# Two hybrid transformer blocks on one core: memory attention that reads its four score banks directly, and an earlier first bias in the differential attention

## The chip, the cores and the metric
One core of a Trainium2 chip runs the whole program in one launch. The metric is the time of one execution on the device in microseconds (us), as the median of several runs. Engines are named as in the profile: PE (matrix products; PEld is its loading of weights), DVE (vector), ACT (scalar functions), POOL and SP (which issues the DMAs of the weights). PE's granted clock is given as a share of 2.4 GHz.

## What is computed
A sequence of 256 tokens with 1024 features goes through two blocks of two layers each, all in float32. The first block ("A") has differential attention, stick-breaking attention and a mixture of product-key experts; the second ("B") has a hybrid attention mixer, cross attention to a memory of 256 tokens, and an MLP. The change touches the softmax of two of these:

```python
# differential attention, per head and block of 128 queries
sc = einsum('bhmqd,bhmkd->bhmqk', dq, dk) * scale
sc = where(dist >= 0, sc - slopes * dist, -inf)
p = softmax(sc, axis=-1)
attn = p[:, :, 0] - lam * p[:, :, 1]
# memory cross attention: 4 heads of 64, no mask and no bias
s = einsum('bqhd,bmhd->bhqm', q, k) * DH ** -0.5
p = softmax(s, axis=-1)
o = einsum('bhqm,bmhd->bqhd', p, v)
```

## The kernel before
All weights come as a stream of tiles of 128 x 2048 values through a ring of four slots. SP loads a slot again when the semaphore `tile_done` says that PE has finished the tile that was in it. Most large products are made of a rounded high part and a low part of each weight: ACT copies a half tile of 1024 columns to `tile_h` (`act_high`), DVE subtracts it and writes the rest over the ring (`dve_low`, one call for the two halves of a tile), and PE adds three products (`pe_project`, `pe_up`, `proj_run`). PE works through its list in a fixed order written by hand; so do ACT and DVE. Semaphores are the only link between them.

Attention is cut into **units**: two heads (or the two maps of one differential head) and 128 queries. Three functions write the three engines' lists for a sequence of units:

- `pe_units` (line 404): the scores of units 0 and 1, then an optional `lead` of other work, then for each unit u: the **turn** (transposes of the probabilities into bank `ps[6]`, L423; it waits for DVE's `sm_p`), the scores of unit u + 2, a piece of **fill** (other products, if there are any), the **values** (probabilities times values; they wait for ACT's copy `pt_ev` of the turned bank), and a second piece of fill. The scores of a unit go to bank 4 or 5 in turn, so those of unit u + 2 wait until the maximum of unit u is there. Between the two halves of a unit's scores PE waits for its own first half (`sc_first`).
- `act_units` (line 444): the exponentials of unit u + 1 (L451: two activations that read S and add up their rows), then the copy of the turned bank of unit u (L465).
- `dve_units` (line 471): for each unit the **bias** (from the bank to the buffer S in SBUF; for a memory unit, which has none, a plain copy, L481) and the maximum over S (L491), then the reciprocal of the sum (L498) and the scaling of the exponentials (`plain_scale`, L509; `diff_scale`, L596 to L598), and an optional `after(u)`. The bias of unit u + 1 is ahead of the scaling of unit u. `step.after` makes DVE wait for its own last result.

There are eight differential units a layer in block A and four memory units a layer in block B. The memory units have no fill: their queries are ready when ACT has copied `ps[4]` to `xq` (L1785), and after the last of them PE goes on with the down product of the memory branch (`down_by_tokens`, L269), once ACT has copied the values' banks 0 and 1 (L1790). That product adds up in banks 0 to 3. Bank 6 holds the turned probabilities, banks 0 and 1 the values.

The differential units have fill: the projections 6 to 9 of the layer's input (`proj_run`, L854), of which six pieces are the `lead`. ACT rounds the tiles 1 to 7 and DVE makes their low parts before the first unit. In `dve_block1` (its loop `for j in range(1, 8)` is ahead of the units) low part 7 and the two small operations for lambda (L1188, L1189) come ahead of the first bias; low parts 8 and 9 come in `after(3)` and `after(5)`. Low part j has to wait for ACT's high part j, and ACT makes high part 7 after it has copied out projection 5.

DVE_A and DVE_B count DVE's own waits in a layer of each block.

Of the kernel before, what the change touches and what calls it, by code (L numbers as in the profile page):

```python
# [125 lines left out]

DVE_A, DVE_B = 128, 121


def program(nc, stream, x_in, consts, table, scratch, out):
    ctx = ExitStack()
    with ctx:
# [266 lines left out]
        sc_mm, sm_max, sm_exp, sm_p = sem("sc_mm"), sem("sm_max"), sem("sm_exp"), sem("sm_p")  # L401
        pt_mm, pt_ev, pv_mm = sem("pt_mm"), sem("pt_ev"), sem("pv_mm")

        def pe_units(pe, base, units, scores, values, fill=None, lead=None):

            def score(u):
                if u >= 2:
                    pe.wait_ge(sm_max, base + (u - 1))
                for m in range(2):
                    klen = units[u]["keys"]  # L410
                    last = scores(units[u], m, ps[4 + u % 2][:, m * 256:m * 256 + klen])
                    if m == 0:
                        last.then_inc(sc_first, 1)
                        pe.wait_ge(sc_first, base + (u + 1))
                last.then_inc(sc_mm, 1)

            def turn(u):
                pe.wait_ge(sm_p, base + (u + 1))
                if u >= 1:
                    pe.wait_ge(pt_ev, base + u)  # L420
                for m in range(units[u]["turned"]):
                    for kt in range(units[u]["keys"] // P):
                        last = nc.tensor.transpose(ps[6][:, (2 * m + kt) * P:(2 * m + kt + 1) * P],  # L423
                                                   E[:, u % 2, m, kt * P:(kt + 1) * P], ident)
                last.then_inc(pt_mm, 1)

            score(0)
            score(1)
            if lead is not None:
                lead()  # L430
            for u in range(len(units)):
                turn(u)
                if u + 2 < len(units):
                    score(u + 2)
                if fill is not None:
                    fill(u, 0)
                pe.wait_ge(pt_ev, base + (u + 1))
                for m in range(2):
                    last = values(units[u], m, PT[:, u % 2, m, :, :])
                last.then_inc(pv_mm, 1)  # L440
                if fill is not None:
                    fill(u, 1)

        def act_units(act, base, units, fill_out=None, after=None):
            def exps(u):
                act.wait_ge(sm_max, base + (u + 1))
                if u >= 2:
                    act.wait_ge(pt_mm, base + (u - 1))
                klen = units[u]["keys"]
                for m in range(2):  # L450
                    last = nc.scalar.activation(E[:, u % 2, m, 0:klen], S[:, u % 2, m, 0:klen], ACT.Exp,  # L451
                                                bias=negmax[:, u % 2, m:m + 1], accum_out=total[:, u % 2, m:m + 1])
                last.then_inc(sm_exp, 1)

            exps(0)
            for u in range(len(units)):
                if u + 1 < len(units):
                    exps(u + 1)
                if fill_out is not None:
                    fill_out(u)  # L460
                act.wait_ge(pt_mm, base + (u + 1))
                if u >= 2:
                    act.wait_ge(pv_mm, base + (u - 1))
                n, maps = units[u]["keys"] // P, units[u]["turned"]
                nc.scalar.activation(PT[:, u % 2, 0:maps, 0:n, :],  # L465
                                     ps[6][:, :].rearrange("p (m k q) -> p m k q", m=2, k=2)[:, 0:maps, 0:n, :],
                                     ACT.Copy).then_inc(pt_ev, 1)
                if after is not None:
                    after(u)

        def dve_units(dve, step, base, units, scale_probs, after=None):
            def bias(u):
                w = units[u]
                klen = w["keys"]
                dve.wait_ge(sc_mm, base + (u + 1))
                if u >= 2:
                    dve.wait_ge(sm_exp, base + (u - 1))
                raw = ps[4 + u % 2][:, :].rearrange("p (m k) -> p m k", m=2)[:, :, 0:klen]
                s = S[:, u % 2, :, 0:klen]
                if w["table"] is None:  # L480
                    last = nc.vector.tensor_copy(s, raw)  # L481
                elif w["minus"] is None:
                    for m in range(2):
                        last = nc.vector.scalar_tensor_tensor(s[:, m, :], raw[:, m, :], w["scale"], w["table"][m],
                                                              ALU.mult, ALU.add)
                else:
                    for m in range(2):
                        last = nc.vector.scalar_tensor_tensor(s[:, m, :], raw[:, m, :], w["minus"][m], w["table"][m],
                                                              ALU.subtract, ALU.add)
                step.after(last)  # L490
                nc.vector.tensor_reduce(negmax[:, u % 2, :], s, AX.X, ALU.max, negate=True).then_inc(sm_max, 1)  # L491
# [678 lines left out]
        def dve_block1(dve, l):  # L1170
# [10 lines left out]
            nc.vector.tensor_reduce(lamp, lam2.rearrange("p (a n) -> p a n", a=2), AX.X, ALU.add).then_inc(lam_sum, 1)  # L1181
            step.after(nc.vector.tensor_scalar(smA[:, 0:1], smA[:, 0:1], smA[:, 2:3], None, ALU.mult))
            dve_split_x(dve, 2 * l)
            for j in range(1, 8):
                dve_low(dve, A_PROJ, l * SPLIT_A - 1, 0, j)
            dve.wait_ge(lam_exp, l + 1)

            step.after(nc.vector.tensor_tensor(neglam, elam[:, 1:2], elam[:, 0:1], ALU.subtract))  # L1188
            step.after(nc.vector.tensor_tensor(neglam, neglam, smA[:, 1:2], ALU.subtract))  # L1189
            def low_after(u):  # L1190
                if u == 3:
                    dve_low(dve, A_PROJ, l * SPLIT_A - 1, 0, 8)
                if u == 5:
# [262 lines left out]
        for pair in range(2):  # L1456
            for qt in range(TT):
                mix_units.append(unit("fox", pair, qt, minus=[negcum[:, qt, 2 * pair + m:2 * pair + m + 1]
                                                              for m in range(2)]))
        mem_units = [unit("mem", pair, qt, keys=SEQ, table=None) for pair in range(2) for qt in range(TT)]  # L1460

        def b_scores(w, m, out):
# [43 lines left out]
        def pe_block2(pe, l):  # L1506
# [150 lines left out]
            arrived(pe, 2, l, B_XQ)  # L1657
            up_as_turned(pe, norm + 1, chunks(B_XQ), 4, lambda: norm_read(pe, norm + 1)).then_inc(tile_done, 1)
            pe.wait_ge(x_ev, l * 3 + 3)
            pe_units(pe, done_b + l * UNITS_B + len(mix_units), mem_units, b_scores, b_values)  # L1660
            pe.wait_ge(xo_ev, l * 2 + 2)
            arrived(pe, 2, l, B_XO)
            down_by_tokens([(slot(B_XO), lambda i, tt: xo[:, i, tt * P:(tt + 1) * P])], True)
# [16 lines left out]
        def act_block2(act, l):  # L1680
# [97 lines left out]
            def memory_out(i):  # L1778
# [5 lines left out]
            finished(act, 2, l, B_XQ)  # L1784
            nc.scalar.activation(xq, ps[4][:, :].rearrange("p (a n) -> p a n", a=2), ACT.Copy,  # L1785
                                 scale=HD ** -0.5).then_inc(x_ev, 1)
            act_units(act, done_b + l * UNITS_B + len(mix_units), mem_units)
            act.wait_ge(pv_mm, done_b + (l + 1) * UNITS_B)
            for b in range(2):
                nc.scalar.activation(xo[:, b, :], ps[b][:, 0:SEQ], ACT.Copy).then_inc(xo_ev, 1)  # L1790
# [7 lines left out]
        def dve_block2(dve, l):  # L1798
# [125 lines left out]
                                        sig[:, i, 2, :], ALU.add).then_inc(br_used, 1)  # L1924
            norm = 2 * LAYERS + 3 * l
            dve_norm(dve, step, norm, 2, l, B_LN1, B_MIX + 3)
            dve_units(dve, step, done_b + l * UNITS_B + len(mix_units), mem_units, plain_scale)
            dve_norm(dve, step, norm + 1, 2, l, B_LN2, B_XO)

            dve_split_x(dve, 2 * LAYERS + 2 * l + 1)  # L1930
# [241 lines left out]
```

## Time and profile before

| | |
|---|---|
| median of 3 runs | 3148.97 us (3147.49 to 3149.35) |
| the profiled execution's own time | 3148.95 us |
| its span, from first to last instruction | 3147.1 us |
| mean granted clock of PE | 0.978 |
| busy: PE, PEld | 3051.5 us (97%), 2638.1 us (84%) |
| busy: DVE, ACT, POOL | 1930.9 us (61%), 1301.5 us (41%), 8.2 us |
| read from HBM | 490 MB, 156 GB/s over the span |

The span is what the timeline covers; the 1.85 us between span and time lie around it. Times in rows are counted from the span's start. A busy PE can still run at half clock, which the busy share doesn't show.

### The profile page before, as it was taken

How to read it: one execution, taken by the hardware profiler on the slowest of the kernel's cores; microseconds unless marked ns; L12 is line 12 of the kernel's file. 1: busy time of each engine (PE TensorE's matmuls, PEld its weight loads, DVE VectorE, ACT ScalarE, POOL GpSimd, SP SyncE). 2: the span in 40 equal slices, each digit the busy share in tenths (PEclk: the TensorE clock that was granted, in tenths of full speed). 3: DMA queues.
4: the chain of work that ended last, by engine and by line, in shares of the span. 5: the costliest groups of instructions: out<-in, count | busy, mean ns of one | idle time of the engine just before them, and what ended most of it. 6: DMA issues, size and time to landing. Idle time of an engine off the chain costs nothing.

```text
span 3147.1 us, 52803 instructions
## 1 busy us (share of the span) xinstructions
PE 3051.5 (97%) x20490; PEld 2638.1 (84%) x20490; DVE 1930.9 (61%) x3611; ACT 1301.5 (41%) x2001; POOL 8.2 (0%) x10
## 2 busy tenths in 40 slices
PE   7999999999999999999999999999998999999898
PEld 7688889898897868888989899797776979777697
DVE  3489864787547548985578755745434564543456
ACT  4422444444444441244444444444424444442444
POOL 0000000000000000000000000000000000000000
PEclk9999999999999999999999999999998999999899
DMA  5244355544545334335553455452243545224354
GB/s 197 94 161 142 127 187 187 188 147 161 194 180 189 146 107 159 133 136 188 186 187 147 170 189 196 175 205 80 81 160 122 187 179 210 81 81 162 119 187 147
DMA packets 68018, 493.53 MB, mean 157 GB/s; under 512 B 7576, under 2 KB 7584, under 8 KB 8352
## 3 DMA queue, kind: packets, MB, share of 16 engines
q1 hardware_dynamic: 67568, 490.42, 43.0%
q8 instruction: 104, 1.70, 0.2%
q0 software_dynamic: 304, 1.06, 0.1%
q14 instruction: 42, 0.34, 0.0%
HBM read 490.39 MB, written 1.06 MB: 156 GB/s over the span
## 4 chain that ended last, share of the span: by engine, by line
PE 93%; DVE 3%; ACT 2%; issue 1%; DMA 0%; DVEq 0%; SPq 0%
PE ps L647 9%; PE ps L649 9%; PE ps L648 9%; PE ps L233 8%; PE ps L617 8%; PE ps L618 8%; PE ps L619 8%; PE ps L699 6%; PE ps L994 3%; PE ps L1008 2%; PE ps L269 2%; PE ps L1607 2%; PE ps L1634 2%; PE ps L250 2%; PE ps L854 1%; PE ps L295 1%
## 5 line engine op out<-in xcount | busy, mean ns | idle before, releaser
L763 DVE TENSOR_TENSOR ring_l<-ring,tile_h 128x1024 fp32r<-128x1024 f32 x648 | 764.8, 1222 | 675.2 <-ACT tile_h L718 671.2
L718 ACT ACTIVATE tile_h<-ring 128x1024 fp32r<-128x1024 f32 x644 | 645.6, 1051 | 533.4 <-PE ps L649 445.3
L617 PE MATMUL ps<-x_h,tile_h 128*128 128x256 f32 x2016 | 575.5, 285 | 0.6 <-issue 0.6
L618 PE MATMUL ps<-x_l,tile_h 128*128 128x256 f32 x2016 | 570.0, 283 | 0.0
L619 PE MATMUL ps<-x_h,ring_l 128*128 128x256 f32 x2016 | 569.9, 283 | 0.0
L617 PEld LDWEIGHTS ps<-x_h,tile_h 128*128 128x128 f32 x2016 | 386.4, 192 | 1.6 <-issue 1.4
L618 PEld LDWEIGHTS ps<-x_l,tile_h 128*128 128x128 f32 x2016 | 386.5, 192 | 0.2
L619 PEld LDWEIGHTS ps<-x_h,ring_l 128*128 128x128 f32 x2016 | 386.3, 192 | 0.0
L722 ACT ACTIVATE arena<-ps 128x512 f32 (+1 forms) x160 | 95.6, 597 | 466.1 <-PE ps L619 345.0
L647 PE MATMUL ps<-tile_h,w_even 128*128 128x512 f32 x640 | 249.5, 390 | 3.6 <-DVE w_even L788 3.6
L647 PE MATMUL ps<-tile_h,w_odd 128*128 128x512 f32 x640 | 249.4, 390 | 0.6 <-DVE w_odd L788 0.6
L648 PE MATMUL ps<-ring_l,w_even 128*128 128x512 f32 x640 | 249.1, 389 | 0.0
L649 PE MATMUL ps<-tile_h,w_odd 128*128 128x512 f32 x640 | 249.0, 389 | 0.0
L649 PE MATMUL ps<-tile_h,w_even 128*128 128x512 f32 x640 | 249.0, 389 | 0.0
L648 PE MATMUL ps<-ring_l,w_odd 128*128 128x512 f32 x640 | 249.0, 389 | 0.0
L233 PE MATMUL ps<-xT,ring 128*128 128x256 f32 x1088 | 237.5, 379 | 0.0
L233 PEld LDWEIGHTS ps<-xT,ring 128*128 128x128 f32 x1088 | 205.5, 190 | 27.3
L784 DVE TENSOR_TENSOR arena<-arena (+1 forms) x160 | 159.9, 1000 | 4.1 <-ACT arena L1142 4.1
L647 PEld LDWEIGHTS ps<-tile_h,w_even 128*128 128x128 f32 x640 | 120.1, 188 | 29.3 <-DVE w_even L788 3.0
L647 PEld LDWEIGHTS ps<-tile_h,w_odd 128*128 128x128 f32 x640 | 120.1, 188 | 27.0 <-issue 2.2
L649 PEld LDWEIGHTS ps<-tile_h,w_even 128*128 128x128 f32 x640 | 120.2, 188 | 25.2
L648 PEld LDWEIGHTS ps<-ring_l,w_odd 128*128 128x128 f32 x640 | 120.2, 188 | 24.9
(305 smaller groups left out, 4988.1 us busy)
## 6 DMA issues: line engine op xcount, KB each, us to landing
ring<-stream SPq DMA_DIRECT2D x464, 1024.0 KB, 4.8
cs<-consts SPq DMA_DIRECT2D x1, 1712.5 KB, 8.5
x<-x_in SPq DMA_DIRECT2D x1, 1024.0 KB, 5.2
arena<-scratch POOLq DMA_DIRECT2D x1, 1024.0 KB, 7.5
out<-x SPq DMA_DIRECT2D x2, 512.0 KB, 2.7
tab<-table SPq DMA_DIRECT2D x1, 1.0 KB, 8.5
scratch<-arena POOLq DMA_DIRECT2D x1, 12.0 KB, 5.9
```

The source lines that it names most:

```text
L233: last = nc.tensor.matmul(ps[bank][:, fb * SEQ:(fb + 1) * SEQ], w[:, c, fb * P:(fb + 1) * P], src[:, c, :], start=(c == 0), stop=(c == KC ...
L617: nc.tensor.matmul(out, uh[:, c, f], x_h[:, c, :], start=(c == 0), stop=False)
L618: nc.tensor.matmul(out, uh[:, c, f], x_l[:, c, :], start=False, stop=False)
L619: ins = nc.tensor.matmul(out, ul[:, c, f], x_h[:, c, :], start=False, stop=(c == KC - 1))
L647: nc.tensor.matmul(out, wh, vh, start=start, stop=False)
L648: nc.tensor.matmul(out, wh, vl, start=False, stop=False)
L649: return nc.tensor.matmul(out, wl, vh, start=False, stop=stop)
L699: ins = nc.tensor.matmul(out, lhs, rhs, start=(c == 0 and m == 0), stop=(c == KC - 1 and m == 2))
L718: nc.scalar.activation(tile_h[:, j % 2, n], slot(k + j)[:, n], ACT.Copy).then_inc(hi_ready, 1)
L722: nc.scalar.activation(hbuf[:, bass.ds(4 * i + j, 1), :].rearrange("p o n -> p (o n)"), ps[4 + j % 2][:, :], func).then_inc(u_act, 1)
L763: nc.vector.tensor_tensor(low_of(k + j)[:, n], slot(k + j)[:, n], tile_h[:, j % 2, n].bitcast(F32), ALU.subtract).then_inc(lo_ready, 1)
L784: nc.vector.tensor_tensor(h2, h2, factor(h2, i, j), ALU.mult).then_inc(u_prod, 1)
```

## The change
Memory units get a list of four banks, 4, 5, 2 and 3. PE issues the scores of all four units, each into its own bank, before the first turn. DVE no longer copies a unit's bank to S: it takes the maximum from the bank, and ACT's exponentials read the bank. The own wait of DVE behind the copy goes, four a layer, so DVE_B falls by 4.

In the differential attention DVE makes low parts 1 and 2, then lambda's two operations, then low parts 3 to 6, and then begins with the units; low part 7 comes behind the scaling of unit 0.

```diff
-DVE_A, DVE_B = 128, 121
+DVE_A, DVE_B = 128, 117
...
-        def pe_units(pe, base, units, scores, values, fill=None, lead=None):
+        def pe_units(pe, base, units, scores, values, fill=None, lead=None, banks=None):
 
             def score(u):
-                if u >= 2:
+                if u >= 2 and banks is None:
                     pe.wait_ge(sm_max, base + (u - 1))
+                bank = ps[4 + u % 2 if banks is None else banks[u]]
                 for m in range(2):
                     klen = units[u]["keys"]
-                    last = scores(units[u], m, ps[4 + u % 2][:, m * 256:m * 256 + klen])
+                    last = scores(units[u], m, bank[:, m * 256:m * 256 + klen])
...
-            score(0)
-            score(1)
+            for u in range(2 if banks is None else len(units)):
+                score(u)
             if lead is not None:
                 lead()
             for u in range(len(units)):
                 turn(u)
-                if u + 2 < len(units):
+                if u + 2 < len(units) and banks is None:
                     score(u + 2)
...
                 for m in range(2):
-                    last = nc.scalar.activation(E[:, u % 2, m, 0:klen], S[:, u % 2, m, 0:klen], ACT.Exp,
+                    raw = S[:, u % 2, m, 0:klen] if banks is None else ps[banks[u]][:, m * 256:m * 256 + klen]
+                    last = nc.scalar.activation(E[:, u % 2, m, 0:klen], raw, ACT.Exp,
                                                 bias=negmax[:, u % 2, m:m + 1], accum_out=total[:, u % 2, m:m + 1])
...
-                raw = ps[4 + u % 2][:, :].rearrange("p (m k) -> p m k", m=2)[:, :, 0:klen]
+                raw = ps[4 + u % 2 if banks is None else banks[u]][:, :]\
+                    .rearrange("p (m k) -> p m k", m=2)[:, :, 0:klen]
+                if banks is not None:
+                    nc.vector.tensor_reduce(negmax[:, u % 2, :], raw, AX.X, ALU.max, negate=True).then_inc(sm_max, 1)
+                    return
                 s = S[:, u % 2, :, 0:klen]
-                if w["table"] is None:
-                    last = nc.vector.tensor_copy(s, raw)
-                elif w["minus"] is None:
+                if w["minus"] is None:
...
-            for j in range(1, 8):
+            for j in range(1, 3):
                 dve_low(dve, A_PROJ, l * SPLIT_A - 1, 0, j)
             dve.wait_ge(lam_exp, l + 1)
 
             step.after(nc.vector.tensor_tensor(neglam, elam[:, 1:2], elam[:, 0:1], ALU.subtract))
             step.after(nc.vector.tensor_tensor(neglam, neglam, smA[:, 1:2], ALU.subtract))
+            for j in range(3, 7):
+                dve_low(dve, A_PROJ, l * SPLIT_A - 1, 0, j)
             def low_after(u):
+                if u == 0:
+                    dve_low(dve, A_PROJ, l * SPLIT_A - 1, 0, 7)
...
+        MEM_BANKS = [4, 5, 2, 3]
```

The calls for the memory units on the three engines pass `banks=MEM_BANKS`.

## Rows read from the trace of the kernel before

**Rows 1.** The page: the chain of work that ended last, by engine.
```profile
PE 93%; DVE 3%; ACT 2%; issue 1%; DMA 0%; DVEq 0%; SPq 0%
```

**Rows 2.** Timeline, memory units of layer 0: start, length, engine, line, operation, [idle before].
```profile
2362.64 2.25 PE L1473 MATMUL ps<-arena 64*128 64x256 f32 x8 [0.69 <-ACT arena L1785]
2364.13 0.69 DVE L481 COPY arena<-ps 128x512 f32<-128x512 f32 x1 [5.91 <-PE ps L1473]
2365.57 0.51 ACT L451 ACTIVATE arena<-arena,negmax 128x256 f32<-128x256 f32 x1 [1.69 <-DVE negmax L491]
2367.64 1.11 PE L423 MATMUL ps<-cs,arena 128*128 128x128 f32 x4 [2.75 <-DVE arena L509]
...
2380.97 1.13 PE L1498 MATMUL ps<-arena 128*64 128x128 f32 x8 [0.69 <-ACT arena L465]
2382.03 1.12 PE L423 MATMUL ps<-cs,arena 128*128 128x128 f32 x4
2383.83 1.13 PE L1498 MATMUL ps<-arena 128*64 128x128 f32 x8 [0.69 <-ACT arena L465]
2385.73 9.67 PE L269 MATMUL ps<-ring,arena 128*128 128x512 f32 x16 [0.77 <-ACT arena L1790]
```

**Rows 3.** Windows, layer 0: length, busy PE, PEld, DVE, ACT, POOL, clock, DMA, GB/s.
```profile
2375.00:2380.00 5.00, 3.77 (x16) 1.94 (x14) 2.48 (x7) 1.25 (x5) 0.00 (x0) 0.50 0.00 0
2386.00:2396.00 10.00, 9.40 (x16) 3.60 (x16) 3.88 (x10) 1.47 (x3) 0.00 (x0) 0.76 0.01 2
```

**Rows 4.** Timeline, first differential units of layer 0, on PE, ACT and DVE.
```profile
54.68 1.61 PE L578 MATMUL ps<-arena 64*128 64x128 f32 x8
58.36 0.28 PE L854 MATMUL ps<-x_h,ring_l 128*128 128x256 f32 x1
61.90 0.33 PE L423 MATMUL ps<-cs,arena 128*128 128x128 f32 x1 [3.27 <-DVE arena L598]
67.46 0.27 PE L423 MATMUL ps<-cs,arena 128*128 128x128 f32 x1
71.45 0.27 PE L423 MATMUL ps<-cs,arena 128*128 128x128 f32 x1
...
55.28 1.99 ACT L718 ACTIVATE tile_h<-ring 128x1024 fp32r<-128x1024 f32 x2
59.99 0.40 ACT L451 ACTIVATE arena<-arena,negmax 128x128 f32<-128x128 f32 x1 [2.72 <-DVE negmax L491]
...
56.36 2.36 DVE L763 TENSOR_TENSOR ring_l<-ring,tile_h 128x1024 fp32r<-128x1024 f32 x2 [3.39 <-ACT tile_h L718]
63.32 0.49 DVE L484 SCALAR_TENSOR_TENSOR arena<-ps,cs 128x128 f32<-128x128 f32 x2 [1.47 <-PE ps L578]
64.75 0.35 DVE L598 SCALAR_TENSOR_TENSOR arena<-arena,rsum 128x128 f32<-128x128 f32 x1
```

**Rows 5.** Windows: behind the first differential turn, at block B's transposes, before memory's fall.
```profile
63.02:66.43 3.41, 3.41 (x17) 3.22 (x16) 1.68 (x7) 0.88 (x4) 0.00 (x0) 0.51 0.03 7
2138.33:2141.74 3.41, 1.91 (x17) 1.22 (x15) 2.95 (x13) 2.88 (x7) 0.00 (x0) 1.00 0.01 2
2363.60:2367.02 3.42, 1.19 (x6) 0.39 (x4) 2.79 (x6) 1.51 (x6) 0.00 (x0) 0.99 0.73 290
```

**Rows 6.** Timeline on PE, the last mixed unit of layer 0.
```profile
2279.59 0.60 PE L423 MATMUL ps<-cs,arena 128*128 128x128 f32 x4
2280.88 0.66 PE L1498 MATMUL ps<-arena 128*64 128x128 f32 x8 [0.32 <-ACT arena L465]
2281.47 0.39 PE L1607 MATMUL ps<-x_h,tile_h 128*128 128x256 f32 x1
```

**Rows 7.** Timeline on PE, the down product behind the memory units of layer 1.
```profile
2936.06 9.28 PE L269 MATMUL ps<-ring,arena 128*128 128x512 f32 x16 [0.77 <-ACT arena L1790]
```

**Rows 8.** Timeline on PE, the first two differential turns of layer 1.
```profile
1070.12 0.47 PE L423 MATMUL ps<-cs,arena 128*128 128x128 f32 x1 [3.27 <-DVE arena L598]
1076.98 0.27 PE L423 MATMUL ps<-cs,arena 128*128 128x128 f32 x1
```

More of the change, by code:

```diff
@@ L442, in pe_units, with act_units @@
                     fill(u, 1)
-        def act_units(act, base, units, fill_out=None, after=None):
+        def act_units(act, base, units, fill_out=None, after=None, banks=None):
             def exps(u):
@@ L469, in act_units, with dve_units @@
                     after(u)
-        def dve_units(dve, step, base, units, scale_probs, after=None):
+        def dve_units(dve, step, base, units, scale_probs, after=None, banks=None):
             def bias(u):
@@ L1659, in pe_block2 @@
             pe.wait_ge(x_ev, l * 3 + 3)
-            pe_units(pe, done_b + l * UNITS_B + len(mix_units), mem_units, b_scores, b_values)
+            pe_units(pe, done_b + l * UNITS_B + len(mix_units), mem_units, b_scores, b_values, banks=MEM_BANKS)
             pe.wait_ge(xo_ev, l * 2 + 2)
@@ L1786, in act_block2 @@
                                  scale=HD ** -0.5).then_inc(x_ev, 1)
-            act_units(act, done_b + l * UNITS_B + len(mix_units), mem_units)
+            act_units(act, done_b + l * UNITS_B + len(mix_units), mem_units, banks=MEM_BANKS)
             act.wait_ge(pv_mm, done_b + (l + 1) * UNITS_B)
@@ L1926, in dve_block2 @@
             dve_norm(dve, step, norm, 2, l, B_LN1, B_MIX + 3)
-            dve_units(dve, step, done_b + l * UNITS_B + len(mix_units), mem_units, plain_scale)
+            dve_units(dve, step, done_b + l * UNITS_B + len(mix_units), mem_units, plain_scale, banks=MEM_BANKS)
             dve_norm(dve, step, norm + 1, 2, l, B_LN2, B_XO)
```

## The prediction
> **What bounds the kernel now.** The page comes first: the chain of work that ended last is 93% PE, and DVE and ACT hold 5% of it between them [rows 1]. So only those places count where PE waits for a softmax, or does its own work at the lower clock. I then read the timeline at the two places that the diff names, and the windows for the granted clock there.
>
> At the memory units of layer 0 the first scores start at 2362.64 and the first turn (the transposes of the probabilities) at 2367.64, after 2.75 us in which PE stood idle; PE then does turn, score, values in a strict order, and reaches the down product of the memory branch (L269) only at 2385.73 [rows 2]. From the first turn that is 18.09 us. Layer 1 has the same pattern. The windows show what else the idle time cost: the clock is 0.50 (1.2 GHz) within the units, and the stretch that holds L269 has a mean of 0.76 [rows 3]. At the differential units of layer 0 PE runs out of work at 58.36 + 0.28 = 58.64 and gets its first turn at 61.90 [rows 4]; the clock is 0.51 in a stretch behind that [rows 5].
>
> The profiled execution took 3148.95 us: a span of 3147.1 and 1.85 around it. The median of the runs is 3148.97, so the sum needs no correction. A difference under 0.2% (6.3 us) counts as no change; that is about what a measurement of this kernel can tell.
>
> **Memory units: the copy goes.** DVE's COPY of a bank to S takes 0.69 us and stands between the first scores and the first exponentials [rows 2]. The maximum now reads the bank itself, and so does the exponential. No row has a maximum over a bank. The COPY row reads the same 512 elements of the same memory on the same engine, so I let the maximum take its 0.69, as it does over S (2364.13 + 0.69 + 0.69 is 2365.51, and the exponential starts at 2365.57). Bounds: half of the COPY less, -0.35, and a second COPY more, +0.69. ACT's exponential of 256 elements in S takes 0.51 [rows 2]; read from a bank I take the same (bounds: -0.1, the step from 128 to 256 elements in rows 2 and 4, and +0.51). So the first turn comes 0.7 us earlier, at 2366.9. The other copies, three a layer, lie beside PE's work of the step before and are worth nothing alone.
>
> **Memory units: four scores at the start.** PE issues the scores of units 2 and 3 right behind 0 and 1, into banks 2 and 3, which nothing uses between the first normalization and L269. Two units' scores took 2.25 us [rows 2]; two more end by 2367.1 at worst, 0.2 behind the first turn's due time. They fill an idle stretch, and I take nothing; if that cover went, they would cost 2.25. After each turn PE goes straight to the values, whose only wait is ACT's copy of the turned bank. The last units before show that short cycle: values at 2380.97, turn at 2382.03, values at 2383.83, so 1.06 + 1.80 = 2.86 us a unit at half clock, and 1.90 from there to L269 [rows 2]. From the first turn to L269: 3 x 2.86 + 1.80 + 1.90 = 12.28, against 18.09: 5.8 less. The softmax keeps up: two exponentials of 0.51 and their sums on ACT, and about as much on DVE, have a whole cycle each.
>
> **What the clock makes of it.** At the full clock the short cycle is in the last of the mixed units: turn 2279.59, values 2280.88, next PE work 2281.47, so 1.29 + 0.59 = 1.88 us a unit [rows 6]. From first turn to L269: 3 x 1.88 + 1.29 + 1.43 (the 1.90 less the 0.47 by which eight values are shorter, 0.66 against 1.13) = 8.36, which is 9.7 less than 18.09. Then L269 too would run at 2.4 GHz: 9.67 us at a mean of 0.76 is 7.3 us of work at full clock, so 2.4 less, and 2.0 less from the 9.28 of layer 1 [rows 2, 3, 7].
>
> Which clock? It fell behind 2.75 us without work (PE busy 1.19 us in the stretch ahead of the fall), while the transposes around 2140, short groups with gaps between them, kept 1.00 with PE busy 1.91 of 3.41 us [rows 2, 5]. After the change PE has a gap of 0.7 in each 1.88, so it is busy nearly two thirds of the time, more like the second. I take the full clock. By the Trainium skill (TensorE: Matmul & The Clock Gate, "A second HAM failure mode: psum-queue depth-cycling") short idles of PE between groups of matmuls, as it cycles through banks, can make the clock fall and rise again. By that rule the units would stay at 1.2 GHz, which is the first rival below; the trace has the fall only behind the longer idle time.
>
> **Sum for memory:** at the full clock 2 x (0.7 + 9.7) + 2.4 + 2.0 = 25.2 us; at half, 2 x (0.7 + 5.8) = 13.0.
>
> **Differential units.** DVE's low part 7 (56.36 to 58.72) stood ahead of the first bias and waited for ACT's high part 7, which ends at 57.27; the scores of both first units began at 54.68 and are done by 56.3 [rows 4]. Now the two biases run beside that high part. What is late next is ACT: its exponential can start when high part 7 ends, at 57.27 instead of 59.99. That is 2.72 us, and the first turn comes at 59.18, 0.54 behind PE's last fill. The low part goes behind the first scaling, to 59.1 to 61.4. Queued behind it on DVE is the bias of unit 2, whose scores would be ready at 63.32 - 2.72 = 60.6: it starts at 61.45, and from bias to end of scaling is 63.32 to 65.10, 1.78 [rows 4]; so the second turn can't come before 63.28. PE's own pace from turn to turn at full clock is 67.46 to 71.45, 4.0 [rows 4], which gives 63.2: a tie, and the low part costs 0.1. PE needs its result only at the second fill of unit 1, some 2.4 us behind that turn. Moving lambda's two small operations ahead of low parts 3 to 6 puts some 0.4 us where DVE waits for ACT anyway; lambda's exponential stands ahead of ACT's second high part: nothing, and 0.4 a layer if that cover were gone. No DMA is added or moved; the ring's loads hang on PE's tile ends and come earlier with them.
>
> The gain at the second turn: layer 0, 67.46 - 63.28 = 4.2. Layer 1 had 1076.98 - 1070.12 = 6.86 from turn to turn, at half clock [rows 8], and gets 4.1: 2.72 + 2.76 = 5.5. Sum 9.7, if an idle time of 0.54 in place of 3.27 leaves the clock up. Bound: with the clock lowered as before, 2 x 2.72 = 5.4.
>
> **Total** 25.2 + 9.7 = 34.9: 3148.95 - 34.9 = 3114.0 us. Everything behind moves forward as a block, since PE bounds it; but each pause at a normalization falls elsewhere, and may gain or lose a stretch at half clock, worth 1.7 us (3.41 at 0.51 [rows 5]). For such places I allow 4 us either way.
>
> **Rivals.**
> 1. The gaps keep PE at 1.2 GHz in the memory units. For it: once down, the clock stayed down through units in which PE was busy more than half the time [rows 3], so one fall at the first unit is enough. Against it: the 1.00 in rows 5. Memory gives 13.0, in all 22.7: 3126.3. Chance 0.31; with one layer of each sort the time lies between.
> 2. The low part is no filler but the wait: DVE comes late to unit 2, PE idles there, the differential part gives nothing, and memory its full gain: 3148.95 - 25.2 = 3123.8. Against it is the tie worked out above. Chance 0.07.
> 3. The edits don't do what they say in time: ACT's and DVE's own order, not the scores, sets the cycle, and under 6.3 us are gained: about 3145. The short cycle in rows 2 speaks against it. Chance 0.03.
> 4. Slower: readings of banks by DVE and ACT, while PE writes others, are held up. Place: the maximum and two exponentials, 0.69 + 2 x 0.51 = 1.7 us on the path of a unit. Even with the half clock they must add (22.7 + 6.3) / 8 = 3.6 us in each of the eight units, over twice their length, to end at 3155 or more. The COPY row, a bank read beside PE's scores, shows nothing of it. Chance 0.01. The Trainium skill (PSUM — Partial Sum Buffer, "Specifications (TRN2)") has both engines reading in parallel at full rate while their banks differ; no row here has both at once.
>
> **The numbers.** The forecast, 3114.0, has 0.58. The range runs from 3107 (the forecast, less the 4 us of placed clock and some 3 of the bounds of the bank readings) to 3130 (rival 1 with its 4 us), and takes in rival 2. Faster by over 0.2%: 0.96 (0.58 + 0.31 + 0.07); within: 0.03; slower: 0.01.
>
> **What would show it.** In the profile after: no COPY; all four units' scores before the first turn; turns about 1.9 us apart (2.9: rival 1), clock 1.00 through the units and L269 in some 7 us; the exponential of the first differential unit right behind high part 7; PE idle about 0.5 us before the first turn, the second 4.1 us behind it. I am wrong if the maximum over a bank takes over 1 us, if the clock falls beside a tighter sequence, or if turns wait for DVE.

## The result, and the profile after

The changed kernel takes **3113.01 us** (median of 4 runs, 3110.59 to 3118.43), the kernel before beside it 3149.16 (4 runs, 3147.49 to 3150.12). The ratio is 0.9888, with a 95% interval of 0.9871 to 0.9905: 1.1% faster, by 36.1 us. The forecast was 3114.0. The profiled execution is the slowest of the four: 3118.43 us, a span of 3116.7, so it shows 30.4 us of the gain.

The page of after, the chain by engine:

```profile
PE 93%; DVE 3%; ACT 2%; issue 1%; DMA 0%; DVEq 0%; SPq 0%
```

PE is still the bound, with the same shares of the chain as in [rows 1].

Timeline of after, memory units of layer 0, on PE, DVE and ACT:

```profile
2351.66 3.84 PE L1482 MATMUL ps<-arena 64*128 64x256 f32 x16 [0.69 <-ACT arena L1794]
2355.79 0.66 PE L424 MATMUL ps<-cs,arena 128*128 128x128 f32 x4 [0.29 <-DVE arena L513]
2357.73 0.66 PE L424 MATMUL ps<-cs,arena 128*128 128x128 f32 x4
...
2364.38 7.13 PE L269 MATMUL ps<-ring,arena 128*128 128x512 f32 x16 [0.77 <-ACT arena L1799]
...
2353.14 1.49 DVE L483 TENSOR_REDUCE negmax<-ps 128x2 f32<-128x512 f32 x2 [5.91 <-PE ps L1482]
2355.65 0.68 DVE L483 TENSOR_REDUCE negmax<-ps 128x2 f32<-128x512 f32 x1
...
2353.87 0.47 ACT L453 ACTIVATE arena<-ps,negmax 128x256 f32<-128x256 f32 x1 [0.96 <-DVE negmax L483]
```

Against [rows 2]: no COPY (DVE's maximum, L483, and ACT's exponential, L453, read the bank); sixteen score products stand in one group; PE's idle time ahead of the first turn is 0.29 instead of 2.75; the turns are 1.94 apart. From the first scores to L269 it takes 2364.38 - 2351.66 = 12.72 us, against 2385.73 - 2362.64 = 23.09.

The same timeline in layer 1, on PE, looks otherwise:

```profile
2889.78 3.84 PE L1482 MATMUL ps<-arena 64*128 64x256 f32 x16 [0.69 <-ACT arena L1794]
2893.92 0.66 PE L424 MATMUL ps<-cs,arena 128*128 128x128 f32 x4 [0.30 <-DVE arena L513]
2896.32 1.12 PE L424 MATMUL ps<-cs,arena 128*128 128x128 f32 x4
2899.18 1.12 PE L424 MATMUL ps<-cs,arena 128*128 128x128 f32 x4
...
2905.74 8.66 PE L269 MATMUL ps<-ring,arena 128*128 128x512 f32 x16 [0.77 <-ACT arena L1799]
```

Here the first turn still takes 0.66, a turn takes 1.12 from the second on, and they are 2.86 apart. The windows tell why (length, busy PE, PEld, DVE, ACT, POOL, clock, DMA, GB/s): layer 0's two stretches, then layer 1's, then the stretch behind the first differential turn of layer 0.

```profile
2351.60:2364.30 12.70, 8.57 (x64) 4.86 (x64) 5.61 (x16) 8.06 (x24) 0.00 (x0) 1.00 0.27 101
2364.30:2372.00 7.70, 7.13 (x16) 2.96 (x16) 3.77 (x9) 1.81 (x4) 0.00 (x0) 1.00 0.01 2
2893.00:2896.00 3.00, 2.02 (x14) 1.37 (x14) 2.67 (x8) 2.31 (x10) 0.00 (x0) 0.87 0.17 68
2896.00:2906.00 10.00, 7.17 (x41) 4.59 (x38) 1.56 (x6) 3.78 (x12) 0.00 (x0) 0.50 0.00 1
...
59.61:63.02 3.41, 3.35 (x27) 3.19 (x26) 3.08 (x9) 0.88 (x4) 0.00 (x0) 1.00 0.03 7
```

In layer 0 the clock is 1.00 (2.4 GHz) all through; in layer 1 it fell to 0.50 (1.2 GHz) behind the first turn and was still down when L269 began. Behind the differential turn it is 1.00, where [rows 5] had 0.51.

Timeline of after, first differential units of layer 0, on PE, ACT and DVE, and PE's turns of layer 1:

```profile
58.88 0.33 PE L424 MATMUL ps<-cs,arena 128*128 128x128 f32 x1 [0.43 <-DVE arena L602]
62.93 0.27 PE L424 MATMUL ps<-cs,arena 128*128 128x128 f32 x1
...
55.09 2.00 ACT L722 ACTIVATE tile_h<-ring 128x1024 fp32r<-128x1024 f32 x2
56.98 0.39 ACT L453 ACTIVATE arena<-arena,negmax 128x128 f32<-128x128 f32 x1
...
55.55 0.49 DVE L488 SCALAR_TENSOR_TENSOR arena<-ps,cs 128x128 f32<-128x128 f32 x2 [2.78 <-PE ps L582]
58.74 2.35 DVE L767 TENSOR_TENSOR ring_l<-ring,tile_h 128x1024 fp32r<-128x1024 f32 x2
...
1062.82 0.33 PE L424 MATMUL ps<-cs,arena 128*128 128x128 f32 x1 [0.43 <-DVE arena L602]
1066.87 0.27 PE L424 MATMUL ps<-cs,arena 128*128 128x128 f32 x1
```

The bias runs beside high part 7, ACT's exponential comes right behind that part, the low part behind the first scaling, and the turns are 4.05 us apart in both layers, where they were 67.46 - 61.90 = 5.56 and 6.86 [rows 4, 8].

**Where the profiled 30.4 us came from.** The same points of the program in the two traces, with the gain reached at each:

```
second differential turn of layer 1   1076.98 -> 1066.87   10.1
memory scores, layer 0                2362.64 -> 2351.66   11.0
end of L269, layer 0                  2395.40 -> 2371.51   23.9   (+12.9)
memory scores, layer 1                2912.97 -> 2889.78   23.2
end of L269, layer 1                  2945.34 -> 2914.40   30.9   (+7.7)
end of the span                       3147.1  -> 3116.7    30.4
```

All of it arises in the two places of the change; from the end of one to the start of the next it moves by under 1 us.

### The profile page after: what moved, and what is told of

Read it like the earlier page. It is cut to its first block, busy times and chain, and to the rows that moved or that the text cites. A ratio compares the mean times of both kernels' runs of the same rounds, so it can differ in the third digit from the quotient of the medians.

```text
span 3116.7 us, 52795 instructions
## 1 busy us (share of the span) xinstructions
PE 3033.5 (97%) x20490; PEld 2629.1 (84%) x20490; DVE 1926.0 (62%) x3603; ACT 1299.1 (42%) x2001; POOL 8.2 (0%) x10
## 4 chain that ended last, share of the span: by engine, by line
PE 93%; DVE 3%; ACT 2%; issue 1%; DMA 0%; DVEq 0%; SPq 0%
PE ps L651 9%; PE ps L653 9%; PE ps L652 9%; PE ps L233 8%; PE ps L621 8%; PE ps L622 8%; PE ps L623 8%; PE ps L703 6%; PE ps L998 3%; PE ps L1012 3%; PE ps L269 2%; PE ps L1616 2%; PE ps L1643 2%; PE ps L250 2%; PE ps L1618 1%; PE ps L295 1%
## 5 line engine op out<-in xcount | busy, mean ns | idle before, releaser
L651 PEld LDWEIGHTS ps<-tile_h,w_even 128*128 128x128 f32 x640 | 120.2, 188 | 29.6 <-DVE w_even L792 3.0
L651 PEld LDWEIGHTS ps<-tile_h,w_odd 128*128 128x128 f32 x640 | 120.1, 188 | 27.0 <-issue 2.2
L653 PEld LDWEIGHTS ps<-tile_h,w_odd 128*128 128x128 f32 x640 | 120.2, 188 | 24.9
```

Of the source, the lines that this page charges most:

```text
L651: nc.tensor.matmul(out, wh, vh, start=start, stop=False)
L653: return nc.tensor.matmul(out, wl, vh, start=False, stop=stop)
```

## The experiments

All kernels are timed beside the kernel before, in three batches, one chip each; it had medians of 3148.48, 3148.19 and 3148.54 there. A ratio is to that kernel of its own batch. Diffs are against the changed kernel, where nothing else is said.

### Each part by itself

**mem_only** keeps the differential part as before:

```diff
-            for j in range(1, 3):
+            for j in range(1, 8):
...
-            for j in range(3, 7):
-                dve_low(dve, A_PROJ, l * SPLIT_A - 1, 0, j)
...
-                if u == 0:
-                    dve_low(dve, A_PROJ, l * SPLIT_A - 1, 0, 7)
```

> Memory part alone, differential part as before. My sum: 25.2 us less than before, 3124, where PE's clock holds through the memory units of both layers; 3136 where it falls in both (rival 1), some 3130 with one of each. The two parts should add up: with the run that has the differential part alone, the two gains together are 36 us, that of the whole change. If the parts help each other through the clock, their sum falls short of it by 3 us or more.

Measured: 3125.89 us (5 runs, 3123.94 to 3129.32), ratio 0.9934 [0.9913, 0.9954], 22.6 us less. Timeline on PE, layer 0:

```profile
2366.62 0.66 PE L424 MATMUL ps<-cs,arena 128*128 128x128 f32 x4 [0.30 <-DVE arena L513]
2368.56 0.66 PE L424 MATMUL ps<-cs,arena 128*128 128x128 f32 x4
...
2375.21 7.13 PE L269 MATMUL ps<-ring,arena 128*128 128x512 f32 x16 [0.77 <-ACT arena L1795]
```

Turns 1.94 apart and L269 in 7.13: full clock, and in layer 1 of this trace as well (turns at 2906.12 and 2908.06). From the first scores to the end of L269 it takes 19.85 us in either layer, where before it took 32.76 and 32.37: 25.4 less together. The profiled execution as a whole is 23.1 us shorter than that of before, so some 2 us were lost elsewhere.

**diff_only** is the kernel before with the differential part alone; this diff is against the kernel before:

```diff
-            for j in range(1, 8):
+            for j in range(1, 3):
...
+            for j in range(3, 7):
+                dve_low(dve, A_PROJ, l * SPLIT_A - 1, 0, j)
             def low_after(u):
+                if u == 0:
+                    dve_low(dve, A_PROJ, l * SPLIT_A - 1, 0, 7)
```

> Differential part alone, memory units as before. My sum: 9.7 us less, 3139.5, with a second turn 4.1 us behind the first in both layers and the clock at 1.00 there. If only the exponentials start earlier and the clock falls as before: 5.4 less, 3143.8. If the low part 7 becomes the wait (rival 2): 3149, with PE idle before the second turn.

Measured: 3137.94 us (10 runs, 3124.59 to 3140.94), ratio 0.9968 [0.9955, 0.9981], 10.5 less; the first two turns at 58.88 and 62.94, so 4.06 apart. The two gains add up to 33.1, beside 36.1 for the whole. With intervals of some 4 and 6 us to either side this is no sign that the parts help each other, and none against it.

### What in the memory part pays: the copy or the order?

**order_only** is mem_only with the copy kept: all scores first, but DVE copies each bank to S and ACT reads S.

```diff
-                    raw = S[:, u % 2, m, 0:klen] if banks is None else ps[banks[u]][:, m * 256:m * 256 + klen]
+                    raw = S[:, u % 2, m, 0:klen]
...
-                    nc.vector.tensor_reduce(negmax[:, u % 2, :], raw, AX.X, ALU.max, negate=True).then_inc(sm_max, 1)
+                    step.after(nc.vector.tensor_copy(S[:, u % 2, :, 0:klen], raw))
+                    nc.vector.tensor_reduce(negmax[:, u % 2, :], S[:, u % 2, :, 0:klen], AX.X, ALU.max,
+                                            negate=True).then_inc(sm_max, 1)
```

> Scores of all four memory units first, in four banks, but the copy to S is kept and maxima and exponentials read S; differential part as before. My theory, that the order of the scores is nearly all of the memory part: 1.4 us slower than the memory part alone where the clock is the same (first turn 0.7 later in each layer), so about 3125.5 with the clock up. Rival, that the removed copy is what counts: about 3149, no gain. Since PE's idle time ahead of the first turn is longer by 0.7 us than without the copy, a fall of the clock is more likely: 3137 then.

Measured: 3122.09 us (4 runs, 3121.56 to 3128.84), ratio 0.992 [0.9897, 0.9944]. Timeline on PE, layer 0:

```profile
2365.31 3.84 PE L1480 MATMUL ps<-arena 64*128 64x256 f32 x16 [0.69 <-ACT arena L1792]
2370.31 0.66 PE L424 MATMUL ps<-cs,arena 128*128 128x128 f32 x4 [1.16 <-DVE arena L515]
2379.11 7.13 PE L269 MATMUL ps<-ring,arena 128*128 128x512 f32 x16 [0.77 <-ACT arena L1797]
```

The order carries the gain. With it PE stands idle only 1.16 us before the first turn, since two more scores fill the wait, the clock holds in both layers, and scores to L269 take 13.80. Without the copy they take 12.72, so the copy's part beside the new order is 1.08 us a layer. Over two layers that is 2.2 us, which the medians of these two kernels (intervals that overlap for the most part) do not resolve; they even stand the other way round.

**banks_only** is the other half: no copy, but the scores of units 2 and 3 behind the turns as before; the differential part is as before too.

```diff
-            for u in range(2 if banks is None else len(units)):
+            for u in range(2):
...
-                if u + 2 < len(units) and banks is None:
+                if u + 2 < len(units):
```

> Maxima and exponentials read four banks, no copy, but the scores of units 2 and 3 come behind the turns as before; differential part as before. My theory: 0.7 us a layer, 3147.7, since the other copies lie beside PE's work, and the cycle stays 5.8 us at half clock. Rival, the copy is on the path of every unit: 8 x 0.69 = 5.5 less, 3143.6. If the shorter idle time alone keeps the clock up: turns come 3.1 us apart in place of 5.8 and 20 us go.

Measured: 3144.47 us (10 runs, 3140.66 to 3146.29), ratio 0.9991 [0.9982, 1.0001]; the interval takes in no change. Timeline on PE, layer 0, and below it the second turn of the kernel before and the copy that stands ahead of it on DVE:

```profile
2367.15 1.05 PE L424 MATMUL ps<-cs,arena 128*128 128x128 f32 x4 [1.89 <-DVE arena L513]
2372.13 1.11 PE L424 MATMUL ps<-cs,arena 128*128 128x128 f32 x4 [0.45 <-DVE arena L513]
...
2383.73 9.11 PE L269 MATMUL ps<-ring,arena 128*128 128x512 f32 x16 [0.77 <-ACT arena L1795]
```

```profile
2373.41 1.11 PE L423 MATMUL ps<-cs,arena 128*128 128x128 f32 x4 [1.17 <-DVE arena L509]
2371.21 0.69 DVE L481 COPY arena<-ps 128x512 f32<-128x512 f32 x1 [3.63 <-PE ps L1473]
```

The clock still falls in both layers, now behind 1.89 us of idle time, as the 1.11 of a turn and the 9.11 of L269 say. But scores to L269 take 20.72 instead of 23.09: 0.86 from the first turn and 1.51 from the second and third turns, which come 4.98 and 5.04 apart instead of 5.77. In the trace of before those turns waited 1.17 us for DVE; here 0.45. The chain behind that wait is the old order itself: DVE's list has the bias (here the copy) of unit 2 ahead of the scaling of unit 1, and the scores of unit 2 came only behind the first turn. So in the old order the copies of units 2 and 3 were on the path as well, against what the prediction said of them.

### Is it the idle time that drops the clock?

**late_turn** keeps everything of the change and makes only the first turn late: DVE sets the unused buffer S to zero three times ahead of the first scaling. That is extra work whose result nothing reads.

```diff
+                if banks is not None and u == 0:
+                    for _ in range(3):
+                        step.after(nc.vector.memset(S.rearrange("p u m k -> p (u m k)"), 0.0))
```

> The changed kernel, but DVE fills the unused buffer S three times (some 2.7 us, its result not used) ahead of the scaling of the first memory unit, so that PE's idle time ahead of the first turn is 3 us again, as in the kernel before, with the new order of the scores. If that idle time is what makes the clock fall: it falls at the first turn in both layers of the profile, turns come 2.86 us apart in place of 1.94, and the time is 2.7 + some 5 us a layer longer than the changed kernel's, 3125. If the clock depends on the order and gaps alone, it holds, and only 2 x 2.7 are added: 3116.

Measured: 3132.34 us (4 runs, 3130.26 to 3133.42), ratio 0.9949 [0.9932, 0.9966]. Timeline on PE and a window, layer 0:

```profile
2359.54 1.11 PE L424 MATMUL ps<-cs,arena 128*128 128x128 f32 x4 [3.88 <-DVE arena L516]
2362.40 1.12 PE L424 MATMUL ps<-cs,arena 128*128 128x128 f32 x4
...
2371.82 9.17 PE L269 MATMUL ps<-ring,arena 128*128 128x512 f32 x16 [0.77 <-ACT arena L1802]
...
2360.00:2370.00 10.00, 7.25 (x42) 4.65 (x42) 2.94 (x11) 4.21 (x12) 0.00 (x0) 0.50 0.00 0
```

PE stands idle for 3.88 us (each memset took 0.91 and a wait of 0.28 ahead of it, so more than the 2.7 that were meant), the clock falls in both layers (in layer 1 the first turn, at 2908.11, takes 1.11 behind the same 3.88), and the turns are 2.86 apart. From first turn to L269 it is 12.28, to the hundredth what the prediction had worked out for the half clock. So an idle stretch ahead of the first turn, with the rest of the change in place, brings rival 1 about in both layers. Against the changed kernel's two medians (3113.0, 3109.4) it costs 19.3 to 23.0: the delay itself is 2 x 3.6 = 7.2 (first turn 7.71 behind the scores instead of 4.13, in both layers), so 12 to 16 are the clock's. The traces say the lower end: from the first scores to the end of L269 it takes 29.16 and 29.64 us, against 19.85 with the clock up, 19.1 more in all and 11.9 without the delay. The prediction had 12.2 between its two cases (25.2 - 13.0). The expectation, 3125, took both terms too small: 2.7 of delay and some 5 of clock a layer, where 3.6 and 6 were measured.

**warm_mem** goes the other way: one product more behind each memory turn, into bank 7, which nothing reads.

```diff
+            def keep(n):
+                for _ in range(n):
+                    nc.tensor.matmul(ps[7][:, 0:256], xT[:, 0, 0:P], xT[:, 1, :], start=True, stop=True)
...
+                if banks is not None:
+                    keep(1)
```

> The changed kernel with one more product (128 x 128 by 256 columns, into the unused bank 7, its result not used) behind each turn of a memory unit, in PE's gap of 0.7 us. If the fall of the clock in the memory units comes from these gaps: clock 1.00 through both layers' units in every profile, and the runs lie near the fast end of the changed kernel, 3111, with less spread. If the clock falls for what PE does ahead of the first turn, it falls as often as without the product, and the time is the same or up to 1 us longer.

Measured: 3112.42 us (6 runs, 3110.16 to 3113.39), ratio 0.989 [0.9874, 0.9906]. The clock holds in both layers and the turns stay 1.94 apart, so the product fits into the wait for ACT's copy, of whose 0.69 us 0.25 are left. Beside it ran **after_again**, the changed kernel as it is:

> The changed kernel once more, as the measure for the three beside it: 3109 to 3119. My theory of its spread: the time differs from one execution to the next by where the clock's stretches fall, above all whether it falls inside the memory units of a layer (5.4 us: L269 is reached 8.4 us after the first turn, or 11.8).

Measured: 3109.37 us (6 runs, 3101.97 to 3118.21), ratio 0.9878 [0.9857, 0.9899]. In its trace the memory units too hold the full clock in both layers. The filling products gain nothing in the median. The runs of warm_mem spread over 3.2 us and those of after_again over 16.2, but that this is the products' work is not shown: the two fastest runs of after_again (3101.97 and 3102.89) lie below all of warm_mem's, and a full clock in the memory units alone does not explain that.

### The low part: filler or wait?

**low_later** moves low part 7 one unit further back, so that nothing stands between the first scaling and the bias of unit 2:

```diff
-                if u == 0:
+                if u == 1:
                     dve_low(dve, A_PROJ, l * SPLIT_A - 1, 0, 7)
```

> The changed kernel, but low part 7 comes behind the scaling of unit 1 in place of unit 0. My working has the low part tied with PE's own pace at the second turn, so only 0.1 us a layer could be gained there; but PE needs the low part at the second fill of unit 1, 2.4 us behind that turn, and now it starts later: at most 1 us a layer either way. If the low part behind unit 0 were what PE waits for (rival 2), this gains 2 us or more a layer.

Measured: 3112.44 us (6 runs, 3108.6 to 3115.46), ratio 0.9892 [0.9875, 0.9909]. Its first turns, timeline on PE:

```profile
56.40 0.33 PE L424 MATMUL ps<-cs,arena 128*128 128x128 f32 x1 [0.43 <-DVE arena L602]
60.46 0.27 PE L424 MATMUL ps<-cs,arena 128*128 128x128 f32 x1
```

4.06 from first to second turn, 4.05 with the low part between, and no wait ahead of the second turn in either: PE's own pace sets both. Rival 2 is out.

**low_first** puts the low part behind the first two biases, ahead of the first scaling:

```diff
+                if u == 0 and first is not None:
+                    first()
...
-            dve_units(dve, step, l * UNITS_A, diff_units, diff_scale, low_after)
+            dve_units(dve, step, l * UNITS_A, diff_units, diff_scale, low_after,
+                      first=lambda: dve_low(dve, A_PROJ, l * SPLIT_A - 1, 0, 7))
```

> The changed kernel, but low part 7 comes behind the first two biases and ahead of the first scaling of the differential units. By my chain (high part 7 ends at 57.0, the low part 1.2 behind it plus 1.1, then reciprocal and scaling 0.95) the first turn comes at 60.3 in place of 58.9, PE is idle 2 us there, and 1.4 us a layer go: 3113 or so. If the clock falls there too, 1.5 to 2.8 us more a layer, up to 3119. If the early bias alone were the gain, nothing changes.

Measured: 3119.0 us (4 runs, 3116.64 to 3119.64), ratio 0.9907 [0.9891, 0.9924]. Timeline on PE, and windows around the first turns of layers 0 and 1:

```profile
58.01 0.33 PE L424 MATMUL ps<-cs,arena 128*128 128x128 f32 x1 [2.08 <-DVE arena L604]
63.58 0.28 PE L424 MATMUL ps<-cs,arena 128*128 128x128 f32 x1
...
59.60:66.40 6.80, 6.74 (x42) 6.26 (x41) 2.87 (x14) 1.72 (x8) 0.00 (x0) 0.75 0.01 2
1064.00:1071.00 7.00, 4.87 (x22) 4.30 (x22) 3.66 (x13) 1.36 (x7) 0.00 (x0) 0.69 0.06 22
```

PE is idle for 2.08 us instead of 0.43, and that is enough for the clock to fall: from the first turn to the second it is 5.57 in place of 4.05. In layer 1 it is 1072.70 - 1066.10 = 6.60, in place of 4.05. The longer idle time is 2 x 1.65, the slower way to the second turn 1.5 + 2.55: 7.4 us in all, and the medians stand 6.0 to 9.6 apart. So the lower clock behind the first turn does hang on the idle time ahead of it, and a good part of the differential part's gain is the clock's.

### Where else the clock is down

PE waits for the normalizations too. The waits of after, PE's row for their transposes (L311 is the transposes, L375 DVE's last step of the normalization; us in total, times, longest):

```profile
PE ps L311 <- DVE x L375: 23.9, 10, 2.8
```

**warm_norms** puts five products between the two token blocks' transposes, into bank 7, which nothing reads; **warm_all** has these and those of warm_mem.

```diff
+                if tt and n is not None and len(tokens) == 2:
+                    for _ in range(5):
+                        nc.tensor.matmul(ps[7][:, 0:256], cs[:, 0:P], cs[:, 0:256], start=True, stop=True)
```

> As the run before, and five such products between the two token blocks' transposes at each normalization without other work in between (2.8 us of idle PE there), so that PE's idle time at seven of them is nearly filled. If the stretches at half clock behind the normalizations come from that idle time, they go: each is worth 1.7 us, in all 8 to 12 us less than the changed kernel, 3102 to 3106. If they come from elsewhere, or the products delay the transposes, the same or up to 5 us longer.

> The changed kernel with the five unused products between the token blocks' transposes at the normalizations alone, none in the memory units. If those stretches are all that the version with both sorts of products gained: the same time as it had, 3098 to 3110, median 3104. If the products in the memory units had a share: slower than it by 2 us or more, with falls in the memory units.

Measured: warm_all 3104.02 us (6 runs, 3098.07 to 3110.73), ratio 0.9868 [0.9847, 0.9889]; warm_norms 3102.51 (4 runs, 3097.28 to 3109.34), ratio 0.9862 [0.9843, 0.9882]. Timeline on PE behind L269 of layer 0, first of the changed kernel, then of warm_norms:

```profile
2376.14 1.78 PE L311 MATMUL ps<-cs,x 128*128 128x128 f32 x8 [2.79 <-DVE x L375]
```

```profile
2358.12 2.32 PE L308 MATMUL ps<-cs 128*128 128x256 f32 x10
2361.08 1.11 PE L314 MATMUL ps<-cs,x 128*128 128x128 f32 x8 [0.64 <-DVE x L378]
```

The products (five, with two records each) fill all but 0.64 of the idle time, and the transposes behind them take 1.11 at full clock, not 1.78. But the largest difference lies elsewhere, in block B of layer 0, some 75 us behind the nearest of these waits. Timeline on PE at that place, two points of the program in after_again, then the same two in warm_norms:

```profile
2099.06 13.61 PE L1542 MATMUL ps<-arena,ring 128*128 128x60 f32 x64 [0.61 <-ACT arena L1702]
2129.26 1.04 PE L1598 MATMUL ps<-cs,arena 128*7 128x128 f32 x8 [1.29 <-DVE arena L1907]
```

```profile
2094.83 7.33 PE L1545 MATMUL ps<-arena,ring 128*128 128x60 f32 x64 [0.61 <-ACT arena L1705]
2115.55 1.04 PE L1601 MATMUL ps<-cs,arena 128*7 128x128 f32 x8 [1.29 <-DVE arena L1910]
```

From the one point to the other it is 30.20 us and 20.72; within that, from 2105 to 2115 in after, the clock was 0.50 (windows in the last section), and in warm_norms it was 1.00 from 2100 to 2130. So 9.5 of the 13.2 us between these two profiled executions (spans of 3109.8 and 3096.6) arise here, and at most the rest at the normalizations. In layer 0 the 64 products of 60 columns take 7.33 in the traces of warm_norms and warm_all and 11.2 to 13.7 in those of all other kernels of this study. By which way products at a normalization reach this place is not shown.

The mean clock of the whole span is 0.995 in warm_norms' profile and 0.985 in after's. The ten runs of warm_all and warm_norms together have a median of 3102.5, the ten of the changed kernel 3111.1: some 8.6 us less, and warm_norms, the simpler one, is the fastest version of this study, 1.4% under the kernel before. The intervals of the two ratios (0.9843 to 0.9882 and, for the changed kernel, 0.9857 to 0.9899) overlap, so the order of the two is likely rather than settled. The products of the memory units add nothing to those of the normalizations: 3104.0 with them, 3102.5 without.

## Why the prediction was right

The forecast was 3114.0 us in a range of 3107 to 3130; 3113.01 was measured. That the two agree to 1 us is in part luck: the same kernel had a median of 3109.37 in another batch. Step by step:

**The copy and the first turn.** Predicted 0.7 earlier, by a maximum of 0.69 over the bank and an unchanged exponential. Measured: the maximum 0.68, the first exponential 0.72 earlier behind the scores (2353.87 - 2351.66 = 2.21, before 2.93), the turn 0.87 earlier (4.13 against 5.00). The other 0.15 come behind the first exponential; the exponentials take 0.46 to 0.48 in place of 0.49 to 0.51.

**"The other copies, three a layer, ... are worth nothing alone" was wrong.** It held that they lie beside PE's work of the step before, and did not look at what the turns waited for. Turns two and three of before had waited 1.17 us for DVE, and banks_only shows 1.5 us a layer for these copies in the old order. The sum was not hurt, since it was made from whole cycles, to which the new order brings DVE in time.

**Four scores at the start** cost nothing: 3.84 us of products end by 2355.5, the turn is due at 2355.79, and what is left of the idle time is 0.29.

**The short cycle.** Predicted 1.88 us a unit and 8.36 from first turn to L269 at full clock; measured 1.94 and 8.59. At half clock 2.86 and 12.28 were predicted; late_turn has both exactly. L269 was to take "some 7": 7.13.

**The clock.** "I take the full clock" held in layer 0 of the profiled run and not in layer 1, so this run shows between the forecast and rival 1, as the rival's text had it. Layer 0 gave 12.9 us where 0.7 + 9.7 + 2.4 = 12.8 were predicted. Layer 1 gave 7.7 where 12.4 were predicted at full clock and 6.5 at half, since its first turn still ran at 1.00. The other six traces with the new order and nothing put into the memory units (after_again, low_later, low_first, mem_only, order_only, warm_norms) have turns of 0.66 us some 1.94 to 2.05 apart in layer 0 and L269 in 7.13 in both layers; with after's own that is one fall in fourteen layers. So the sum rests on the right case, and the profiled run was 5 us over the median for a reason of which its own layer 1 gives 4.7. The reason argued was that gaps of 0.7 us are not 2.75 us of idle time. For the place ahead of the first turn the runs bear it out: the clock fell in both layers behind 3.88 (late_turn), 2.75 (before) and 1.89 us (banks_only), and in neither behind 1.16 (order_only).

The sentence "the trace has the fall only behind the longer idle time" holds for the memory units and not for the trace as a whole. The trace of before also has a fall behind a short one, in block B of layer 0, by its timeline and windows:

```profile
2109.97 12.96 PE L1533 MATMUL ps<-arena,ring 128*128 128x60 f32 x64 [0.61 <-ACT arena L1693]
...
2105.00:2110.00 5.00, 4.39 (x41) 4.28 (x39) 0.30 (x1) 1.19 (x3) 0.00 (x0) 1.00 0.59 203
2110.00:2115.00 5.00, 5.00 (x28) 5.00 (x29) 3.60 (x9) 4.91 (x9) 0.00 (x0) 0.60 0.93 331
```

PE was busy 4.39 of 5 us there and had waited 0.61. So rival 1, a fall without long idle time, had more for it than the prediction gave it.

Why the clock fell in layer 1 of after is open: the 0.30 before the first turn and the 0.69 before each values group are the same there as in layer 0. The rule of the Trainium skill (TensorE: Matmul & The Clock Gate, "A second HAM failure mode: psum-queue depth-cycling") describes such falls beside short idles; the traces agree in that they can occur here, and not in that they are the usual case.

**The differential units.** First turn predicted at 59.18, measured 58.88; the scores there started 0.19 earlier too (54.49, before 54.68). Predicted idle 0.54, measured 0.43. Second turn 4.1 behind it, measured 4.05 in both layers, and with the low part moved away 4.06: the tie that the prediction found. (Its own terms, 61.45 + 1.78, give 63.23 and not 63.28, which changes nothing.) The clock stayed up, as taken; low_first shows what 2.08 us of idle time would have done. Up to layer 1's second turn 10.1 us were gained, where the sum had 9.7.

**The total.** 34.9 predicted; 30.4 in the profiled run, 35.1 if its layer 1 had held the clock, 36.1 between the medians.

**The term for placed clock stretches** (4 us either way) was too small for single executions. The kernel before alone ran from 3133.2 to 3151.3 in one batch, and the changed one from 3101.97 to 3118.21. For medians of a few runs it was enough.

**Rivals.** 1 came true in one layer of one trace. 2 is refuted by low_later. 3 and 4 are refuted by the time itself; the bank readings cost nothing (maximum 0.68, exponential 0.47 while PE wrote other banks, and while the other of the two engines read one: the second maximum and the first exponential of layer 0 overlap).

## What to carry to other kernels

When PE waits ahead of a row of small units, ask first whether work from later units can be issued into that wait: here four scores in four banks took nearly all the gain of the memory part, and taking the copy away without it 2.4 us a layer in the trace and nothing that the medians settle. Much of what an idle stretch costs may not be in the stretch but behind it, at half the clock, so price a removed wait twice, once at each level, and look in the windows for the fall. Where a wait can't be removed, unused products in an unused bank are worth a try, with several runs of each version, since single executions of one kernel lay up to 16 us apart here, and with a look at where in the trace the gain arises.

## What the runs showed of the hardware

**A reading of a bank is not dearer.** ACT's exponential of 256 elements took 0.47 us from the bank and 0.51 from S; DVE's maximum over 512 took 0.68 from the bank and 0.69 from S.

**The clock can stay down while PE is hardly ever idle.** Windows of after, block B of layer 0:

```profile
2105.00:2110.00 5.00, 5.00 (x25) 5.00 (x25) 0.93 (x3) 1.32 (x2) 0.00 (x0) 0.50 0.57 213
2110.00:2115.00 5.00, 5.00 (x29) 4.41 (x28) 1.38 (x2) 0.87 (x5) 0.00 (x0) 0.50 0.37 120
```

Two stretches of 5 us with PE busy all through, at 1.2 GHz. Most of the work there is the 64 products of 60 columns (L1542), which take 12.93 us from 2098.85 on. In warm_norms' trace this place holds the full clock in layer 0 and not in layer 1, where the stretch from 2630 to 2640 has 10.00 us of PE busy at 0.50. What keeps it down was not tested.

**Two groups of times.** Of the ten runs of warm_all and warm_norms five lie between 3097.28 and 3098.46 and four between 3109.34 and 3110.73, with one at 3106.6. Something of about 11 us is there or not in an execution. Both traces of these kernels are of the faster group, so what it is stays open. The stretch just shown is of that size (9.5 us between after_again's trace and warm_norms'), and in both traces the clock held through it in layer 0; that it makes the two groups was not seen.
